# The first attention unit moved into the last block of the input projection

## The chip, the core and the metric

The kernel runs on one core of a Trainium2 chip. The time is the device time of one execution in microseconds; a smaller one is better. Engines: PE is TensorE (PEld its weight loads), DVE is VectorE, ACT is ScalarE, POOL is GpSimd, SP is SyncE, which here only issues DMAs.

## What is computed

One trunk layer of a diffusion model for 512 latent and 128 context tokens with 2048 channels: an input projection of 4608 columns, differential attention (8 heads) and grouped-query attention (8 heads on 2 key heads), an output projection, and 16 experts chosen by the experts. What matters here is the projection and the attention:

```python
p = jnp.einsum('bnd,de->bne', h, w_in)
dq, dk, dv, gq, gk, gv = jnp.split(p, splits, axis=-1)
gq = rmsnorm(gq.reshape(b, n, N_GQA_HEADS, HEAD_DIM), qn_g)
...
a1 = jax.nn.softmax(jnp.einsum('bqhd,bkhd->bhqk', qb1, k1).astype(jnp.float32) * scale, axis=-1)
a2 = jax.nn.softmax(jnp.einsum('bqhd,bkhd->bhqk', qb2, k2).astype(jnp.float32) * scale, axis=-1)
a = (a1 - lam * a2).astype(v.dtype)
return jnp.einsum('bhqk,bkhd->bqhd', a, v)
```

## The kernel before

The tokens are five tiles of 128 (four latent, `TL = 4`, and one of context). The **input projection** runs over nine blocks of 512 columns in the order `ORDER = [8, 2, 3, 4, 0, 1, 6, 7, 5]`: keys first, then queries; block 5, the last, holds values. A block has 16 steps `k`, one for each 128 input channels. A step is 15 matmuls: for each of the five token tiles three products of high and low parts (`three_products`), added up in PSUM banks 0 to 4. Bank 5 serves sums of the conditioning, banks 6 and 7 take transpositions in turn (`xp_bank`).

After a block, ScalarE copies the five banks to `prow` (`block_out`; for block 5 to `V`). VectorE shapes these rows: for blocks 6 to 8 it first sums squares (`mean_squares`, step kind "squares"), GpSimd turns the sums into `rg` by a power, and then `shape_rows` scales and rotates tile by tile (step kind "shape") and counts `roped`. TensorE transposes the shaped rows, four heads of a tile at a time (step kind "rows", line 992), and ScalarE copies them into `qT` or `kT` (line 1435). All of this is laid out by hand in one list of steps, `make_steps()`, that each engine walks through in its own order, with semaphores between them. In block `o`, "shape" of the former block's tile `t` stands at step `2t + 1`, and "rows" of tile `t` follows step `6 + 2t`:

```python
            if o > 0 and ORDER[o - 1] in ROWS_BLOCKS and k >= 6 and k % 2 == 0:
                steps.append(("rows", ORDER[o - 1], (k - 6) // 2))
```

TensorE waits for `roped` ahead of these transpositions. The weights of the projection come in pieces of four steps by SyncE (line 795), are rounded by ScalarE (line 1407) and completed by VectorE (line 2018, "split"); the last piece is asked for after step 7 of the last block.

**Attention** has 68 units, differential (even) and grouped-query ones (odd) in turn. A unit is: `scores` (TensorE, line 1025), `maxima` (VectorE, lines 2047 and 2048), `exps` (ScalarE, line 1454, two for a differential unit), `combine` (VectorE, lines 2083 to 2087, which joins the two maps; 2079 for the others), `prob_transposes` (TensorE, lines 1039 and 1044, into banks 5 and 6), a copy (ScalarE, lines 1507 and 1509), and `values` (TensorE, line 1063, into bank 7). Scores of differential units lie in banks 0 to 3, those of the others in banks 3 and 4. Scores stand two units ahead:

```python
            pe.wait_ge(proj_taken, NT * len(ORDER))
            pe.wait_ge(mod_copied, len(GROUPS))
            scores(0)
            scores(1)
            for u in range(UNITS):
                if u + 2 < UNITS:
                    scores(u + 2)
                ...
                if u >= 1:
                    values(u - 1)
                prob_transposes(u)
```

`scores(u)` from unit 2 on waits until the exponentials of unit `u - 2` are done. The exponentials of unit 0 go to `E`, whose first half lies over two of the three places of the rounded weights.

Of the kernel before, what the change touches and what calls it, by code (L numbers as in the profile page):

```python
# [41 lines left out]
P = 128  # L42
# [56 lines left out]
RAW_AT = {3: (0,), 4: (1,), 5: (2,), 6: (3, 4)}  # L99
ROUTER_AT = {5: (0,), 7: (1, 2)}  # L100
# [63 lines left out]
def make_steps():  # L164
# [37 lines left out]
    for o, b in enumerate(ORDER):  # L202
        for k in range(12 if o == 0 else 0, KC):
# [24 lines left out]
            if o > 0 and ORDER[o - 1] in ROWS_BLOCKS and k >= 6 and k % 2 == 0:  # L228
                steps.append(("rows", ORDER[o - 1], (k - 6) // 2))
# [54 lines left out]
def build(nc, a, laid, outs):  # L284
# [6 lines left out]
    with ctx:  # L291
# [417 lines left out]
        def unit(u):  # L709
            t, j = SEQ[u]  # L710
            nc_, keys = (2 if j < DH else 1), (LAT + PAST if t < TL else 4 * CTX)
            kh = j if j < DH else DH + (j - DH) // GRP
            scale = (DQ if j < DH else HD) ** -0.5
            return t, j, nc_, keys, kh, scale

        def is_diff(u):
            return SEQ[u][1] < DH

        def is_four(u):
            return SEQ[u][0] == TL  # L720

        def four_heads(u):
            return range(SEQ[u][1], SEQ[u][1] + 4)
# [4 lines left out]
        def four_scores(u):  # L728
            n = 8 if is_diff(u) else 4
            return S_ps(u, 0, CTX * n).rearrange("p (h k) -> p h k", k=CTX)  # L730
# [27 lines left out]
        def S_ps(u, c, keys):  # L758

            at0 = S_STEP * c if is_diff(u) else 3 * NB  # L760
            return ps[:, at0:at0 + keys]

        def S_both(keys):
            return ps[:, 0:2 * S_STEP].rearrange("p (c k) -> p c k", c=2)[:, :, 0:keys]
# [103 lines left out]
        def _(pe):  # L868
# [5 lines left out]

            pe.wait_ge(ident_ready, 1)
            for step in STEPS:
                kind = step[0]
                if kind == "cvec":
# [117 lines left out]
            def four_scored(u):  # L996
                _, _, comps, _, _, _ = unit(u)
                qs, ks = slice(P * TL, P * NT), slice(LAT + PAST, LAT + PAST + CTX)
                for i, j in enumerate(four_heads(u)):
                    for c in range(comps):  # L1000
                        rows = slice(0, HD) if comps == 1 else slice(DQ * c, DQ * (c + 1))
                        mm = pe.matmul(four_scores(u)[:, 4 * c + i, :], qT[rows, j, qs], kT[rows, key_head(j), ks],
                                       start=True, stop=True, skip_group_check=True)
                mm.then_inc(scored, 1)

            def scores(u):
                t, j, comps, keys, kh, _ = unit(u)
                if u >= 2:
                    pe.wait_ge(exp_done, u - 1)
                if is_four(u):  # L1010
                    four_scored(u)
                    return
                k0 = 0
                qs = slice(P * t, P * (t + 1))
                if comps == 1:
                    parts = [(0, 0, LAT), (0, LAT, keys)]
                else:

                    parts = [(0, LAT, keys), (1, LAT, keys), (0, 0, 384), (1, P, LAT), (0, 384, LAT), (1, 0, P)]
                for n, (c, lo, hi) in enumerate(parts):  # L1020
                    if n == 5:

                        pe.wait_ge(tail_scored, TAILS[u])
                    rows = slice(0, HD) if comps == 1 else slice(DQ * c, DQ * (c + 1))
                    mm = pe.matmul(S_ps(u, c, keys)[:, lo:hi], qT[rows, j, qs], kT[rows, kh, k0 + lo:k0 + hi],  # L1025
                                   start=True, stop=True, skip_group_check=True)
                    if n == 0 and comps == 2:
                        mm.then_inc(tail_scored, 1)
                mm.then_inc(scored, 1)

# [46 lines left out]
            was_taken(pe, XP_TOTAL - 2)  # L1077
            was_taken(pe, XP_TOTAL - 1)
            pe.wait_ge(proj_taken, NT * len(ORDER))
            pe.wait_ge(mod_copied, len(GROUPS))  # L1080
            scores(0)
            scores(1)
            for u in range(UNITS):
                if u + 2 < UNITS:
                    scores(u + 2)
                if u in OT_AT:
                    pe.wait_ge(pt_copied, u)
                    out_transposes(*OT_AT[u], bank(6))
# [3 lines that stand above are left out]
# [249 lines left out]
        def _(act):  # L1341
# [32 lines left out]

            for step in STEPS:
                kind = step[0]
                if kind == "lam":
# [67 lines left out]
            def exps(u):  # L1445
                t, j, comps, keys, _, scale = unit(u)
                act.wait_ge(max_done, u + 1)
                if u >= 2:
                    act.wait_ge(pt_done, u - 1)
                if is_four(u):  # L1450
                    act.activation(four_probs(u), four_probs(u), ACT.Exp, scale=scale).then_inc(exp_done, 1)
                    return
                for c in range(comps):
                    ins = act.activation(E[:, u % 2, c, 0:keys], S_ps(u, c, keys), ACT.Exp,
                                         bias=nmax[:, u % 4, c:c + 1], scale=scale,
                                         accum_out=ssum[:, u % 4, c:c + 1])
                ins.then_inc(exp_done, 1)

# [36 lines left out]
            exps(0)  # L1495
# [307 lines left out]
        def _(dve):  # L1803
# [115 lines left out]

            for step in STEPS:  # L1920
                kind = step[0]
                if kind == "half":
# [115 lines left out]
            def maxima(u):  # L2038
                t, j, comps, keys, _, scale = unit(u)
                dve.wait_ge(scored, u + 1)  # L2040
                if u >= 1:
                    dve.wait_ge(max_done, u)
                if is_four(u):
                    link(dve.tensor_reduce(four_stats(u)[0], four_scores(u), AX, ALU.max))
                    return
                S = S_both(keys) if comps == 2 else S_ps(u, 0, keys).rearrange("p (c k) -> p c k", c=1)
                link(dve.tensor_reduce(mx[:, 0:comps], S, AX, ALU.max))  # L2047
                dve.tensor_scalar(nmax[:, u % 4, 0:comps], mx[:, 0:comps], -scale, None, ALU.mult).then_inc(max_done, 1)

            def four_shifted(u):  # L2050

                dve.wait_ge(pt_done, u - 1)
                dve.tensor_tensor(four_probs(u), four_scores(u), bc(four_stats(u)[0], CTX, 2), ALU.subtract)\
                    .then_inc(max_done, 1)

            def four_combine(u):

                probs = four_probs(u)
                _, total, inverse, factor = four_stats(u)
                dve.wait_ge(exp_done, u + 1)  # L2060
                dve.wait_ge(probs_ready, u)
                link(dve.tensor_reduce(total, probs, AX, ALU.add))
                if not is_diff(u):
                    dve.reciprocal(inverse, total).then_inc(probs_ready, 1)
                    return
                link(dve.reciprocal(inverse, total))
                link(dve.scalar_tensor_tensor(out=factor, in0=total[:, 0:4], scalar=neglam[:, 0:1], in1=inverse[:, 4:8],
                                              op0=ALU.mult, op1=ALU.mult))
                link(dve.tensor_tensor(probs[:, 4:8, :], probs[:, 4:8, :], bc(factor, CTX, 2), ALU.mult))
                dve.tensor_tensor(probs[:, 0:4, :], probs[:, 0:4, :], probs[:, 4:8, :], ALU.add).then_inc(probs_ready, 1)  # L2070

            def combine(u):
                t, j, comps, keys, _, _ = unit(u)
                if is_four(u):
                    four_combine(u)
                    return
                dve.wait_ge(exp_done, u + 1)
                if comps == 1:
                    dve.reciprocal(rsum[:, u % 4, 0:1], ssum[:, u % 4, 0:1]).then_inc(probs_ready, 1)
                    return  # L2080
                if u >= 1:
                    dve.wait_ge(probs_ready, u)
                link(dve.reciprocal(rsum[:, u % 4, :], ssum[:, u % 4, :]))
                link(dve.scalar_tensor_tensor(out=coef[:, :], in0=ssum[:, u % 4, 0:1], scalar=neglam[:, 0:1],
                                              in1=rsum[:, u % 4, 1:2], op0=ALU.mult, op1=ALU.mult))

                dve.scalar_tensor_tensor(out=E[:, u % 2, 0, 0:keys], in0=E[:, u % 2, 1, 0:keys], scalar=coef[:, 0:1],
                                         in1=E[:, u % 2, 0, 0:keys], op0=ALU.mult, op1=ALU.add).then_inc(probs_ready, 1)

# [37 lines left out]
            maxima(0)  # L2127
            maxima(1)
            combine(0)
# [368 lines left out]
```

## Time and profile before

| | us |
|---|---|
| median of 3 runs | 2104.59 |
| lowest, highest | 2102.16, 2107.1 |
| the profiled execution | 2109.96 |
| its span in the trace | 2108.1 |
| TensorE busy | 2029.9 (96%) |
| VectorE, ScalarE busy | 1140.6, 478.1 |
| mean granted clock of TensorE | 0.989 |

The span runs from the first to the last instruction; the execution's own time is 1.9 us longer. Projection and attention are the first 810 us; the output projection and the routing follow until about 1090, then the experts to the end. An engine's idle time counts only where TensorE stands for it. A row of a timeline gives the start, the duration of one instruction or of a merged group, the engine, the line, and in brackets the idle time before it with what ended it. Matmuls overlap: one of 512 columns lasts 0.39 us, and the next starts 0.23 later. A granted clock of 1.00 is 2.4 GHz, one of 0.50 is 1.2 GHz.

### The profile page before, as it was taken

The page shows a single profiled execution, that of the slowest core. Times are in us where ns is not written, and L with a number is a line of the kernel's source. Part 1 is how long each engine was busy: PE and PEld are TensorE (multiplying, and loading weights), DVE is VectorE, ACT ScalarE, POOL GpSimd, SP SyncE. Part 2 cuts the span into 40 slices and gives each one's busy share as a digit, 9 for nine tenths or more (in the row PEclk, how much of TensorE's full clock was granted, in tenths as well). Part 3 has the DMA queues.
Part 4 walks back from the last instruction along what each step waited for, and adds up shares of the span by engine and source line. Part 5 has one row for each costly group of instructions (what it writes and reads, how often), then busy time and mean ns, then how long its engine had stood idle before and what let it go on. Part 6 is the DMA issues. An engine that isn't in the chain of part 4 may idle for free. (4 is left out here: it accounts for less than half of the span.)

```text
span 2108.1 us, 37671 instructions
## 1 busy us (share of the span) xinstructions
PE 2029.9 (96%) x15045; PEld 1128.7 (54%) x15045; DVE 1140.6 (54%) x2673; ACT 478.1 (23%) x846; POOL 163.3 (8%) x236
## 2 busy tenths in 40 slices
PE   6999999999999999999979999999999999999995
PEld 3578888787878887888842333333333333333331
DVE  4369988997448877777355342333233333223314
ACT  4232222222247776221210000000000000000003
POOL 1020011111000001111120000000000000000001
PEclk9999999999999999999989999999999999999998
DMA  9955567562220005656489999999999999999997
GB/s 389 410 181 219 215 229 259 198 219 101 80 103 1 1 2 221 226 182 207 146 306 378 404 412 418 416 416 425 422 416 416 418 416 414 430 415 417 417 394 312
DMA packets 71924, 614.03 MB, mean 291 GB/s; under 512 B 8432, under 2 KB 10104, under 8 KB 29104
## 3 DMA queue, kind: packets, MB, share of 16 engines
q1 hardware_dynamic: 47392, 514.36, 59.1%
q0 software_dynamic: 18672, 84.89, 12.8%
q10 hardware_dynamic: 5776, 13.63, 1.9%
q8 instruction: 56, 0.92, 0.2%
q14 instruction: 28, 0.23, 0.0%
HBM read 583.28 MB, written 29.60 MB: 291 GB/s over the span
## 5 line engine op out<-in xcount | busy, mean ns | idle before, releaser
L1250 PE MATMUL ps<-arena 128*32 128x512 f32 x6144 | 662.6, 592 | 0.2 <-DVE arena L2301 0.2
L1250 PEld LDWEIGHTS ps<-arena 128*32 128x32 f32 x6144 | 199.4, 110 | 458.3 <-issue 457.7
L1277 PE MATMUL ps<-arena 128*32 128x512 f32 x3072 | 332.8, 592 | 3.7 <-DMA arena<-in_w_expert 1.9
L697 PE MATMUL ps<-B_w_hi,B_x_hi 128*128 128x512 f32 x720 | 287.0, 399 | 6.2 <-DVE B_x_lo L2030 3.3
L699 PE MATMUL ps<-B_w_lo,B_x_hi 128*128 128x512 f32 x720 | 281.5, 391 | 0.0
L698 PE MATMUL ps<-B_w_hi,B_x_lo 128*128 128x512 f32 x720 | 281.3, 391 | 0.0
L1277 PEld LDWEIGHTS ps<-arena 128*32 128x32 f32 x3072 | 99.6, 110 | 234.1 <-issue 227.7
L2333 DVE COPY arena<-arena 128x16 f32 x1200 | 157.3, 182 | 99.9 <-issue 99.1
L2309 DVE TENSOR_TENSOR arena<-ps,arena 64x256 f32<-64x256 f32 x96 | 39.9, 416 | 295.9 <-ACT arena L1605 295.2
L1605 ACT ACTIVATE arena<-ps 64x512 f32<-64x512 f32 x48 | 28.5, 593 | 608.8 <-PE ps L1250 608.8
L697 PEld LDWEIGHTS ps<-B_w_hi,B_x_hi 128*128 128x128 f32 x720 | 135.5, 188 | 47.3 <-issue 12.7
L699 PEld LDWEIGHTS ps<-B_w_lo,B_x_hi 128*128 128x128 f32 x720 | 135.5, 188 | 29.1
L698 PEld LDWEIGHTS ps<-B_w_hi,B_x_lo 128*128 128x128 f32 x720 | 135.8, 189 | 26.7
L1900 DVE SCALAR_TENSOR_TENSOR arena<-arena,cT 128x2048 f32<-128x2048 f32 x60 | 138.2, 2345 | 2.3 <-DMA arena<-in_w_mod 2.3
L1407 ACT ACTIVATE B_w_hi<-arena 128x1024 fp32r<-128x1024 f32 x72 | 75.5, 1058 | 264.7 <-DMA arena<-in_w_in_b 237.3
L2345 DVE COPY arena<-ps 16x512 f32<-16x512 f32 x30 | 20.8, 692 | 208.4 <-PE ps L1277 208.2
L697 PE MATMUL ps<-D_w_hi,D_oT_hi 128*128 128x512 f32 x320 | 126.8, 396 | 0.2 <-DVE D_oT_lo L2125 0.2
L699 PE MATMUL ps<-D_w_lo,D_oT_hi 128*128 128x512 f32 x320 | 124.9, 390 | 0.0
L2018 DVE TENSOR_TENSOR B_w_lo<-arena,B_w_hi 128x1024 fp32r<-128x1024 f32 x72 | 87.7, 1219 | 68.5 <-ACT B_w_hi L1407 68.3
L698 PE MATMUL ps<-D_w_hi,D_oT_lo 128*128 128x512 f32 x320 | 124.6, 390 | 0.0
L2185 DVE SCALAR_TENSOR_TENSOR arena<-arena,cT 128x512 f32<-128x512 f32 x120 | 82.6, 745 | 29.2 <-DMA arena<-in_w_mod 29.1
L2047 DVE TENSOR_REDUCE mx<-ps 128x2 f32<-128x1280 f32 (+1 forms) x64 | 74.0, 1156 | 44.8 <-PE ps L1025 44.1
(286 smaller groups left out, 1964.9 us busy)
## 6 DMA issues: line engine op xcount, KB each, us to landing
arena<-in_w_expert SPq DMA_DIRECT2D x192, 2048.0 KB, 13.9
arena<-in_w_in_b SPq DMA_DIRECT2D x36, 1024.0 KB, 4.9
arena<-in_w_mod_q SPq DMA_DIRECT2D x32, 1024.0 KB, 19.2
arena<-in_w_mod POOLq DMA_DIRECT2D x32, 1024.0 KB, 5.6
arena<-in_w_mod POOLq DMA_DIRECT2D x32, 512.0 KB, 4.6
arena<-in_w_out_b SPq DMA_DIRECT2D x16, 1024.0 KB, 7.0
arena<-in_w_mod POOLq DMA_DIRECT2D x64, 256.0 KB, 3.5
arena<-in_x_sample SPq DMA_DIRECT2D x8, 1024.0 KB, 10.2
```

The costliest lines, as they stand in the source:

```text
L697: eng.matmul(out, x_hi, w_hi, start=start, stop=False)
L698: eng.matmul(out, x_lo, w_hi, start=False, stop=False)
L699: return eng.matmul(out, x_hi, w_lo, start=False, stop=stop)
L1250: mm = pe.matmul(bank(g)[32 * q:32 * q + 32, :], e_rows, w[q], start=start, stop=stop, skip_group_check=True)
L1277: mm = pe.matmul(bank(b)[32 * q:32 * q + 32, :], hT[g][:, f, :], w_four[q], start=f == 0, stop=f == 7, skip_group_check=True)
L1407: act.activation(w_hi, raw, ACT.Copy).then_inc(w_hi_ready, 1)
L1900: ins = dve.scalar_tensor_tensor(out=macs[:, v, :], in0=at(where, D), scalar=cT[:, k, v:v + 1], in1=macs[:, v, :], op0=ALU.mult, op1=ALU.add)
L2018: dve.tensor_tensor(w_lo, raw, w_hi.bitcast(F32), ALU.subtract).then_inc(w_lo_ready, 1)
L2047: link(dve.tensor_reduce(mx[:, 0:comps], S, AX, ALU.max))
L2185: ins = dve.scalar_tensor_tensor(out=late_acc[:, v, :], in0=piece, scalar=cT[:, k, v:v + 1], in1=late_acc[:, v, :], op0=ALU.mult, op1=ALU.add)
L2309: ins = dve.tensor_tensor(hid[g][64 * c:64 * (c + 1), :], bank(g)[0:64, cs], sg[g][0:64, cs], ALU.mult)
L2333: ins = dve.tensor_copy(xstage[:, :, c + i:c + i + 1], x1_cols[:, bass.ds(place, 1), :].rearrange("p o k -> p k o"))
```

## The change

`first_unit`, a new kind of step, stands after step 13 (`FIRST_UNIT_K`) of the last block. There TensorE issues the scores of unit 0, VectorE its maximum and combination, ScalarE its exponentials. The scores of unit 0 go to banks 5 to 7, at the same distance of the two maps as before. So that these banks are free, the transpositions of the former block's rows follow steps 4, 6, ... 12 of the last block; in the other blocks they stay. The functions `four_scored`, `scores`, `exps`, `maxima`, `combine` and their like are moved ahead of the loop over the steps, unchanged. After the block, TensorE transposes the probabilities of unit 0 first, then waits for the bank copies, then issues the scores of units 1 and 2.

```diff
+FIRST_UNIT_K = 13
...
-            if o > 0 and ORDER[o - 1] in ROWS_BLOCKS and k >= 6 and k % 2 == 0:
-                steps.append(("rows", ORDER[o - 1], (k - 6) // 2))
+            first_row = 4 if o == len(ORDER) - 1 else 6
+            if o > 0 and ORDER[o - 1] in ROWS_BLOCKS and k in range(first_row, first_row + 2 * NT, 2):
+                steps.append(("rows", ORDER[o - 1], (k - first_row) // 2))
+            if (o, k) == (len(ORDER) - 1, FIRST_UNIT_K):
+                steps.append(("first_unit",))
...
-            at0 = S_STEP * c if is_diff(u) else 3 * NB
+            at0 = (5 * NB if u == 0 else 0) + S_STEP * c if is_diff(u) else 3 * NB
...
-        def S_both(keys):
-            return ps[:, 0:2 * S_STEP].rearrange("p (c k) -> p c k", c=2)[:, :, 0:keys]
+        def S_both(u, keys):
+
+            at0 = S_STEP - LAT - P if u == 0 else 0
+            from_ = 5 * NB - at0 if u == 0 else 0
+            return ps[:, from_:from_ + 2 * S_STEP].rearrange("p (c k) -> p c k", c=2)[:, :, at0:at0 + keys]
...
+                if kind == "first_unit":
+                    was_taken(pe, XP_TOTAL - 2)
+                    was_taken(pe, XP_TOTAL - 1)
+                    pe.wait_ge(mod_copied, len(GROUPS))
+                    scores(0)
...
-            was_taken(pe, XP_TOTAL - 2)
-            was_taken(pe, XP_TOTAL - 1)
+            prob_transposes(0)
             pe.wait_ge(proj_taken, NT * len(ORDER))
-            pe.wait_ge(mod_copied, len(GROUPS))
-            scores(0)
             scores(1)
-            for u in range(UNITS):
+            scores(2)
+            for u in range(1, UNITS):
...
+                if kind == "first_unit":
+                    after_products(act, len(ORDER) - 1, FIRST_UNIT_K)
+                    exps(0)
...
-            exps(0)
             for u in range(UNITS):
...
+                if kind == "first_unit":
+                    maxima(0)
+                    combine(0)
...
-            maxima(0)
             maxima(1)
-            combine(0)
```

## Rows read from the trace of the kernel before

**Rows 1.** Busy time by stretch (us, busy by engine with instructions, PEclk, DMA share, GB/s).

```profile
core 0: us, PE busy (x) PEld busy (x) DVE busy (x) ACT busy (x) POOL busy (x), PEclk, DMA share, GB/s
...
599.08:611.33 12.25, 9.09 (x53) 6.48 (x52) 6.90 (x14) 5.81 (x15) 1.14 (x2) 0.86 0.42 139
611.33:805.00 193.67, 192.97 (x1519) 160.43 (x1519) 156.91 (x324) 140.34 (x357) 9.08 (x9) 1.00 0.01 1
```

**Rows 2.** TensorE timeline, last block: step 5 begins; rows after 6, 8; last matmul.

```profile
559.27 0.39 PE L697 MATMUL ps<-B_w_hi,B_x_hi 128*128 128x512 f32 x1
...
566.07 0.60 PE L992 MATMUL ps<-ident,arena 128*128 128x128 f32 x4
...
573.35 0.60 PE L992 MATMUL ps<-ident,arena 128*128 128x128 f32 x4
...
598.85 0.39 PE L699 MATMUL ps<-B_w_lo,B_x_hi 128*128 128x512 f32 x1
```

**Rows 3.** Timelines of GpSimd, VectorE and ScalarE in the same block.

```profile
557.07 4.43 POOL L1646 TENSOR_TENSOR rg<-ssg,mhalf 128x20 f32<-128x20 f32 x1 [52.56 <-DVE ssg L1835]
...
563.76 0.69 DVE L1868 TENSOR_TENSOR arena<-arena 128x512 f32<-128x512 f32 x1
...
579.32 0.69 DVE L1868 TENSOR_TENSOR arena<-arena 128x512 f32<-128x512 f32 x1
...
574.97 1.06 ACT L1407 ACTIVATE B_w_hi<-arena 128x1024 fp32r<-128x1024 f32 x1 [7.66 <-DMA arena<-in_w_in_b]
```

**Rows 4.** Timelines of VectorE and TensorE in the block before it, tile 0.

```profile
506.76 0.69 DVE L1868 TENSOR_TENSOR arena<-arena 128x512 f32<-128x512 f32 x1
...
507.60 0.63 PE L992 MATMUL ps<-ident,arena 128*128 128x128 f32 x4 [0.39 <-DVE arena L1868]
```

**Rows 5.** Timeline of all engines where attention begins.

```profile
600.12 2.64 PE L1025 MATMUL ps<-arena 64*128 64x128 f32 x16 [0.89 <-ACT arena L1357]
...
601.59 1.49 DVE L2047 TENSOR_REDUCE mx<-ps 128x2 f32<-128x1280 f32 x1 [19.12 <-PE ps L1025]
...
603.32 0.79 ACT L1454 ACTIVATE arena<-ps,nmax 128x640 f32<-128x640 f32 x1 [3.45 <-DVE nmax L2048]
...
605.03 2.51 PE L1025 MATMUL ps<-arena 64*128 64x128 f32 x12 [2.27 <-ACT arena L1454]
...
607.47 0.98 PE L1039 MATMUL ps<-ident,arena 128*128 128x128 f32 x4
...
608.40 1.25 PE L1025 MATMUL ps<-arena 128*128 128x512 f32 x4
```

**Rows 6.** Timelines of TensorE and VectorE over one steady pair of units.

```profile
617.26 1.36 PE L1025 MATMUL ps<-arena 64*128 64x128 f32 x12
...
618.55 1.38 PE L1063 MATMUL ps<-arena 128*128 128x128 f32 x10
...
619.77 0.60 PE L1039 MATMUL ps<-ident,arena 128*128 128x128 f32 x4
...
620.32 1.25 PE L1025 MATMUL ps<-arena 128*128 128x512 f32 x4
...
621.40 1.32 PE L1063 MATMUL ps<-arena 128*128 128x128 f32 x10
...
621.60 0.82 DVE L2047 TENSOR_REDUCE mx<-ps 128x1 f32<-128x640 f32 x1 [0.91 <-PE ps L1025]
...
622.46 0.15 DVE L2048 TENSOR_SCALAR nmax<-mx 128x1 f32<-128x1 f32 x1
...
623.20 1.14 PE L1025 MATMUL ps<-arena 64*128 64x128 f32 x8
```

**Rows 7.** Busy time in single microseconds at the beginning of attention.

```profile
605.00:606.00 1.00, 0.97 (x6) 0.93 (x8) 0.92 (x3) 0.75 (x2) 0.00 (x0) 0.50 0.60 242
```

**Rows 8.** TensorE in the routing stage: timeline, and busy time of one stretch.

```profile
1079.82 1.03 PE L1212 MATMUL ps<-ident,arena 64*64 64x16 f32 x8 [9.27 <-DVE arena L2258]
...
1082.63:1086.05 3.42, 3.42 (x18) 3.42 (x18) 1.74 (x9) 0.00 (x0) 2.45 (x4) 0.50 0.25 53
```

More of the change, by code:

```diff
@@ L873, in xp_bank, with four_scored, scores @@
                 return bank(6 + i % 2)
+            def four_scored(u):
+                _, _, comps, _, _, _ = unit(u)
+                qs, ks = slice(P * TL, P * NT), slice(LAT + PAST, LAT + PAST + CTX)
+                for i, j in enumerate(four_heads(u)):
+                    for c in range(comps):
+                        rows = slice(0, HD) if comps == 1 else slice(DQ * c, DQ * (c + 1))
+                        mm = pe.matmul(four_scores(u)[:, 4 * c + i, :], qT[rows, j, qs], kT[rows, key_head(j), ks],
+                                       start=True, stop=True, skip_group_check=True)
+                mm.then_inc(scored, 1)
+            def scores(u):
+                t, j, comps, keys, kh, _ = unit(u)
+                if u >= 2:
+                    pe.wait_ge(exp_done, u - 1)
+                if is_four(u):
+                    four_scored(u)
+                    return
+                k0 = 0
+                qs = slice(P * t, P * (t + 1))
+                if comps == 1:
+                    parts = [(0, 0, LAT), (0, LAT, keys)]
+                else:
+                    parts = [(0, LAT, keys), (1, LAT, keys), (0, 0, 384), (1, P, LAT), (0, 384, LAT), (1, 0, P)]
+                for n, (c, lo, hi) in enumerate(parts):
+                    if n == 5:
+                        pe.wait_ge(tail_scored, TAILS[u])
+                    rows = slice(0, HD) if comps == 1 else slice(DQ * c, DQ * (c + 1))
+                    mm = pe.matmul(S_ps(u, c, keys)[:, lo:hi], qT[rows, j, qs], kT[rows, kh, k0 + lo:k0 + hi],
+                                   start=True, stop=True, skip_group_check=True)
+                    if n == 0 and comps == 2:
+                        mm.then_inc(tail_scored, 1)
+                mm.then_inc(scored, 1)
             pe.wait_ge(ident_ready, 1)
@@ L877, in _ @@
                 kind = step[0]
-                if kind == "cvec":
+                if kind == "first_unit":
[3 more added lines that the diff above has]
+                    scores(0)
+                elif kind == "cvec":
                     pe.wait_ge(c_in, 32)
@@ L993, in _ @@
                     mm.then_inc(xp_done, 1)
[L996 to L1029, printed above, removed]
             def prob_transposes(u):
@@ L1373, in block_out, with exps @@
                             act.dma_start(dv_d[P * t:P * (t + 1), :], prow[:, t, :]).then_inc(val_out, 16)
+            def exps(u):
+                t, j, comps, keys, _, scale = unit(u)
+                act.wait_ge(max_done, u + 1)
+                if u >= 2:
+                    act.wait_ge(pt_done, u - 1)
+                if is_four(u):
+                    act.activation(four_probs(u), four_probs(u), ACT.Exp, scale=scale).then_inc(exp_done, 1)
+                    return
+                for c in range(comps):
+                    ins = act.activation(E[:, u % 2, c, 0:keys], S_ps(u, c, keys), ACT.Exp,
+                                         bias=nmax[:, u % 4, c:c + 1], scale=scale,
+                                         accum_out=ssum[:, u % 4, c:c + 1])
+                ins.then_inc(exp_done, 1)
             for step in STEPS:
                 kind = step[0]
-                if kind == "lam":
+                if kind == "first_unit":
+                    after_products(act, len(ORDER) - 1, FIRST_UNIT_K)
+                    exps(0)
+                elif kind == "lam":
                     act.wait_ge(lam_sum, 1)
@@ L1442, in _ @@
                                    ACT.Copy).then_inc(xp_taken[i % 2], 1)
[L1445 to L1457, printed above, removed]
             def take_ot(i, b):
@@ L1918, in half_sum, with maxima @@
                     ins.then_inc(mac_done[v], 1)
+            def maxima(u):
+                t, j, comps, keys, _, scale = unit(u)
+                dve.wait_ge(scored, u + 1)
+                if u >= 1:
+                    dve.wait_ge(max_done, u)
+                if is_four(u):
+                    link(dve.tensor_reduce(four_stats(u)[0], four_scores(u), AX, ALU.max))
+                    return
+                S = S_both(u, keys) if comps == 2 else S_ps(u, 0, keys).rearrange("p (c k) -> p c k", c=1)
+                link(dve.tensor_reduce(mx[:, 0:comps], S, AX, ALU.max))
+                dve.tensor_scalar(nmax[:, u % 4, 0:comps], mx[:, 0:comps], -scale, None, ALU.mult).then_inc(max_done, 1)
@@ new lines, in four_shifted, with four_combine @@
+            def four_shifted(u):
+                dve.wait_ge(pt_done, u - 1)
+                dve.tensor_tensor(four_probs(u), four_scores(u), bc(four_stats(u)[0], CTX, 2), ALU.subtract)\
+                    .then_inc(max_done, 1)
+            def four_combine(u):
+                probs = four_probs(u)
+                _, total, inverse, factor = four_stats(u)
+                dve.wait_ge(exp_done, u + 1)
+                dve.wait_ge(probs_ready, u)
+                link(dve.tensor_reduce(total, probs, AX, ALU.add))
+                if not is_diff(u):
+                    dve.reciprocal(inverse, total).then_inc(probs_ready, 1)
+                    return
+                link(dve.reciprocal(inverse, total))
+                link(dve.scalar_tensor_tensor(out=factor, in0=total[:, 0:4], scalar=neglam[:, 0:1], in1=inverse[:, 4:8],
+                                              op0=ALU.mult, op1=ALU.mult))
+                link(dve.tensor_tensor(probs[:, 4:8, :], probs[:, 4:8, :], bc(factor, CTX, 2), ALU.mult))
+                dve.tensor_tensor(probs[:, 0:4, :], probs[:, 0:4, :], probs[:, 4:8, :], ALU.add).then_inc(probs_ready, 1)
@@ new lines, in combine @@
+            def combine(u):
+                t, j, comps, keys, _, _ = unit(u)
+                if is_four(u):
+                    four_combine(u)
+                    return
+                dve.wait_ge(exp_done, u + 1)
+                if comps == 1:
+                    dve.reciprocal(rsum[:, u % 4, 0:1], ssum[:, u % 4, 0:1]).then_inc(probs_ready, 1)
+                    return
+                if u >= 1:
+                    dve.wait_ge(probs_ready, u)
+                link(dve.reciprocal(rsum[:, u % 4, :], ssum[:, u % 4, :]))
+                link(dve.scalar_tensor_tensor(out=coef[:, :], in0=ssum[:, u % 4, 0:1], scalar=neglam[:, 0:1],
+                                              in1=rsum[:, u % 4, 1:2], op0=ALU.mult, op1=ALU.mult))
+                dve.scalar_tensor_tensor(out=E[:, u % 2, 0, 0:keys], in0=E[:, u % 2, 1, 0:keys], scalar=coef[:, 0:1],
+                                         in1=E[:, u % 2, 0, 0:keys], op0=ALU.mult, op1=ALU.add).then_inc(probs_ready, 1)
@@ L1920, in _ @@
             for step in STEPS:
                 kind = step[0]
-                if kind == "half":
+                if kind == "first_unit":
+                    maxima(0)
+                    combine(0)
+                elif kind == "half":
                     half_sum(step[1])
@@ L2035, in _ @@
                     shape_rows(step[1], step[2])
[L2038 to L2088, printed above, removed]
```

## The prediction

> **What bounds the kernel now.** I read the engine shares first, then the busy time by stretch, then the timelines around the edit. The page gives TensorE 96% of the span, so what moves the end is time in which TensorE stands or runs at half clock. By stretch there is one such place at the edit: in the 12.25 us from the end of the last projection step to the scores of unit 4, TensorE is busy for 9.09 us at a mean granted clock of 0.86, while over the rest of attention it is busy for 192.97 of 193.67 us [rows 1]. In the last projection block itself it does not wait once: step follows step every 3.40 us ((566.07 - 559.27) / 2), with four transpositions of the former block's rows between some of them [rows 2]. So whatever is put into that block is paid in full, unless something there is removed, and any wait there is new time.
>
> **Boundary, before.** The last product is issued at 598.85, so the block ends at 599.08 (one matmul pitch is 0.23). scores(0) waits for the copies out of the five banks and starts at 600.12. The maximum starts at 601.59, the exponentials at 603.32, and scores(2), which waits for the exponentials of unit 0, starts at 605.03 [rows 5]. scores(0) and scores(1) are issued in 1.29 + 1.08 = 2.37 us at full clock [rows 6], so TensorE stands from 602.49 to 605.03. Idle in all: 1.04 + 2.54 = 3.58 us. The clock is at 0.50 from 605 on [rows 7]: scores(2) takes 2.44 instead of 1.29 us, the transpositions of unit 0 0.93 instead of 0.55 [rows 5, 6]. That is 1.53 us more. Idle and clock together are 5.1 of the 12.25 us.
>
> **Boundary, after.** I lay the new order out from the same durations, with the block's end still written as 599.08. Transpositions of unit 0: to 599.63. Wait for the bank copies, as before: to 600.12. scores(1): to 601.20. scores(2), free of its wait, since exponentials 0 are done: to 602.49. scores(3) waits for the exponentials of unit 1: maximum from 601.40, 1.01 us with its scaling, exponential from about 602.44, 0.85 long ((605.03 - 603.32) / 2), so scores(3) starts at about 603.38 and ends at 604.46. Values of unit 0 and transpositions of unit 1 (1.22 + 0.60) bring it to 606.28. scores(4) needs exponentials 2: the maximum of unit 2 starts at 602.49 + 0.18, the exponentials 1.73 later, done 1.71 after that, at 606.1 [rows 5, 6]. So scores(4) starts at 606.28 and the steady beat of 5.94 us a pair follows. From block's end to scores(4): 7.20 us, against 12.25. scores(0) is moved, not removed: inside the block it costs its 1.29 us and I add 0.1 for its seams. **Gain: 12.25 - 7.20 - 1.39 = 3.7 us.** It rests on the clock staying up, with 0.49 + 0.89 = 1.4 us idle in place of 3.58.
>
> **What the moved unit does in the block.** Same 12 matmul records, one maximum, two exponentials, one combination; other banks (5 to 7), same shapes. After step 13 come 6.8 us of products; the chain of unit 0 takes 0.18 + 1.73 + 1.71 us to the exponentials and about 1.3 to the combination, 4.9 in all, so it is hidden, with 1.9 us to spare. ScalarE is done at 3.6 us, before the first bank is ready for copying at about 4.3 (3.40 + 0.68 + latency), so the copies queued behind the exponentials are not late. VectorE has nothing else queued there. The waits added on TensorE (two copies of turned rows, the last modulation copy) have long been met: the last rows now come after step 12, a whole step earlier. SyncE's loads of V and of the output weights hang on steps 11 and 15 and only move with them; GpSimd's stores likewise.
>
> **The rows steps.** To make room, the five transposition steps of block 7's rows move from after steps 6, 8, ... 14 to after steps 4, 6, ... 12. This is the term that decides. The rows of tile 0 must be shaped first, and this chain does not hang on TensorE at that point: GpSimd raises the mean squares to a power from 557.07 to 561.50, VectorE shapes behind it, and its last addition runs 563.76 to 564.45 [rows 3]. The transpositions started at 566.07, 1.6 us later, without a wait. After the change their place is the end of step 4, 559.27 [rows 2]. They can start at 564.60: in the block before, the same handoff, with its transpositions after step 6, is just reached, TensorE waits 0.39 us and starts 0.15 after the addition ends (506.76 + 0.69 = 507.45, start 507.60) [rows 4]. So TensorE stands for 564.60 - 559.27 = **5.33 us**, with steps 5 and on queued behind it. Nothing gives it back: no later wait in the block can shrink, since there is none. The other tiles are in time: tile 3, the closest, is shaped 10.06 us after the end of step 7 (579.32 + 0.69, against 573.35 - 3.40 = 569.95), because its shaping queues behind a weight piece that lands 5.02 us after that step [rows 2, 3]; its new place comes 3 x 3.40 + 0.48 = 10.68 after it (0.48 is what four transpositions add, 573.35 - 566.07 - 2 x 3.40). With 0.15 for the start that leaves some 0.5 us; a slower landing would add up to about 1 us.
>
> **The clock after that wait** is not shown by the trace of before at this place. Lower bound: after idle of 1.04 and 2.54 us the clock fell once and cost 1.53 us [rows 5, 7]. Upper bound: after a 9.27 us wait in the routing stage it stays at 0.50 from 1079.82 to 1086.05 with TensorE at work again [rows 8], 6.2 us of which half, 3.1 us, is lost. The wait of 5.33 lies between; nearer to the first, so I take **2.0 us**. (Zero is excluded: the idle here is longer than the one that made it fall.)
>
> **Sum:** + 5.33 + 2.0 - 3.7 = **+3.6 us**. The profiled execution took 2109.96 us (span 2108.1 and 1.9 around it) and would take 2113.6; it lay 5.4 above the median of the runs. I put the same difference on the median: 2104.6 + 3.6 = **2108.2 us**. The stages behind attention start later by the same amount and have no load that is timed from anything earlier.
>
> **Rivals.** (A, my forecast, chance 0.62) as above, +2.5 to +5 us. (B, 0.08) The clock is hardly lower after the wait, contrary to the rows: +5.3 + 0.2 - 3.7 = +1.8. (C, 0.14) A further loss: the clock falls again at the start of attention, where two idle pieces remain (1.53), or tile 3's rows are late (up to 1): +4.6 to +6. For: the two pieces lie within 4.3 us. Against: 1.4 us is much less than 3.58. (D, the other side, 0.10) No wait at tile 0: the shaping is ready in time, and only the gain is left, 2104.6 - 3.7 = 2100.9 us. It decides if tile 0's last addition ends by about 559.1, 5.3 us earlier than in the trace; GpSimd's power alone ends at 561.50 [rows 3], so it needs a misreading of mine. (E, 0.06) The change does not do what it says: unit 0 is ahead, but scores(3) hangs on unit 1's exponentials by the same chain, and the stand of 2.54 us is only passed on. Then only the first 1.04 us and part of the clock are won, about 2: +5.3. Against: in the layout scores(2) and the transpositions fill that chain's time.
>
> For C a rule speaks beside the rows. Transpositions of unit 0 run between the two idle pieces, and in the steady beat, with ten transpositions a pair, the clock stays at 1.00 [rows 1]. The Trainium skill, "TensorE: Matmul & The Clock Gate", Part 4, says that a transposition does not count as busy for the clock as a matmul does. By it the idle at the start of attention would look like 2.0 instead of 1.4 us, still below 3.58; were it to make the clock fall, the sum would be +5.1. The trace can't show it at this place; it is part of why C has 0.14.
>
> **Chances.** A measurement of this kernel tells some 0.2%, 4.2 us, from no change. A lies across that bound: of its 0.62 I give 0.38 to within and 0.24 to slower. B is within. C: 0.02 within, 0.12 slower. D is a gain of 0.18%: 0.06 within, 0.04 faster. E slower. Together faster 0.04, within 0.54, slower 0.42. Range: A, B and C with the spread of the runs of before (2102.2 to 2107.1, about 2.5 to a side) give 2104.2 to 2112.0; D is left out below.
>
> **What would show it.** Right: the transpositions of block 7's first rows start with an idle of about 5.3 us released by VectorE's last shaping addition, and the clock is at half for some us behind it; the exponentials of unit 0 lie inside the block; scores(2) follows scores(1) without a wait; from block's end to scores(4) 7.2 us. Wrong: no wait there (D); a low clock again at the start of attention or a wait at tile 3's rows (C); 2 us or more of idle before scores(3) (E).

## The result

| | us |
|---|---|
| before, median of 22 runs | 2105.22 (2101.86 to 2109.29) |
| changed, median of 22 runs | 2110.20 (2106.91 to 2115.41) |
| ratio | 1.0020, interval 1.0014 to 1.0026 |
| forecast | 2108.2 (2104.2 to 2112.0) |

The change makes the kernel slower by 0.20%, 4.2 us by the ratio (2.9 to 5.5); + 3.6 was forecast. The forecast's 2108.2 stands on 2104.59, the median of the three runs of before that were at hand; over 22 runs it is 2105.22. In the profiled execution TensorE waits at the place that the forecast names, and for what it names. Timeline of TensorE, then VectorE and GpSimd, in the last projection block of the changed kernel (start, duration, engine, line, operation, in brackets the idle time before and what ended it); the lines answer to [rows 2] and [rows 3]:

```profile
555.00 0.39 PE L703 MATMUL ps<-B_w_lo,B_x_hi 128*128 128x512 f32 x1
...
560.47 1.02 PE L1039 MATMUL ps<-ident,arena 128*128 128x128 f32 x4 [5.08 <-DVE arena L1880]
...
569.38 0.60 PE L1039 MATMUL ps<-ident,arena 128*128 128x128 f32 x4
```

```profile
552.94 4.43 POOL L1658 TENSOR_TENSOR rg<-ssg,mhalf 128x20 f32<-128x20 f32 x1 [52.47 <-DVE ssg L1847]
...
559.63 0.69 DVE L1880 TENSOR_TENSOR arena<-arena 128x512 f32<-128x512 f32 x1
```

The last product of step 4 is issued at 555.00, so the step ends at 555.23. VectorE's last addition for tile 0 runs 559.63 to 560.32, and the transpositions start 0.15 us behind it. By starts the wait is 5.24 us. The next transpositions follow 8.91 us after these, where [rows 2] has 7.28 for the same work. The busy time by stretch (columns as in [rows 1]; the clock is the number behind POOL) shows why: the clock is at half behind the wait.

```profile
561.40:562.40 1.00, 1.00 (x4) 0.81 (x4) 0.96 (x3) 0.60 (x1) 0.00 (x0) 0.50 0.06 16
562.40:563.40 1.00, 1.00 (x3) 0.73 (x3) 1.00 (x3) 0.00 (x0) 0.00 (x0) 0.50 0.00 0
563.40:564.40 1.00, 1.00 (x5) 0.80 (x4) 0.74 (x2) 0.00 (x0) 0.00 (x0) 0.71 0.00 0
603.43:610.64 7.21, 6.28 (x42) 4.35 (x40) 3.90 (x9) 4.17 (x11) 1.14 (x2) 1.00 0.73 236
```

The last of these lines is the beginning of attention, from the block's end to the scores of unit 4: 7.21 us at a clock of 1.00, against 12.25 us at 0.86 in [rows 1]. Its timeline, with the moved unit's scores ahead of it, answers to [rows 5]:

```profile
595.20 1.36 PE L911 MATMUL ps<-arena 64*128 64x128 f32 x12
...
596.61 1.49 DVE L1941 TENSOR_REDUCE mx<-ps 128x2 f32<-128x1280 f32 x1 [10.89 <-PE ps L911]
...
598.40 0.80 ACT L1394 ACTIVATE arena<-ps,nmax 128x640 f32<-128x640 f32 x1 [5.94 <-DVE nmax L1942]
...
600.55 0.88 DVE L1981 SCALAR_TENSOR_TENSOR arena<-arena,coef 128x640 f32<-128x640 f32 x1
...
603.43 0.60 PE L1051 MATMUL ps<-ident,arena 128*128 128x128 f32 x4
...
604.27 2.64 PE L911 MATMUL ps<-arena 128*128 128x512 f32 x16
...
607.70 1.35 PE L911 MATMUL ps<-arena 128*128 128x512 f32 x4 [0.79 <-ACT arena L1394]
...
610.64 1.36 PE L911 MATMUL ps<-arena 64*128 64x128 f32 x12
```

Unit 0 is scored at 595.20, its maximum starts at 596.61, the combination ends at 601.43, 2.0 us before its transpositions at 603.43. Scores of units 1 and 2 then run in one piece (x16), and scores(3) stands 0.79 us for the exponentials of unit 1.

Spans don't show the difference: the changed kernel's profiled execution has 2106.9 us, the one before 2108.1. Both kernels are the same up to the last block, yet GpSimd's power (the one instruction that turns the sums of squares into `rg`) starts at 552.94 in one and at 557.07 in the other. So I compare traces by one stretch, **from the start of GpSimd's power in the last block (line 1646 before) to the first matmul of the scores of unit 4**. It holds all that the change touches. Before: 611.33 - 557.07 = 54.26 us. Changed: 610.64 - 552.94 = 57.70. Difference: + 3.44 us. The measure is not exact: over the traces of this case step 4 of the last block ends 2.00 to 2.34 us after the power starts, so two stretches compare to some 0.3 us.

### The profile page after: what moved, and what is told of

Its sections match the earlier page's. It is cut to its first block and busy times, and to the rows that moved or that the text cites. A ratio compares the mean times of both kernels' runs of the same rounds, so it can differ in the third digit from the quotient of the medians.

```text
span 2106.9 us, 37670 instructions
## 1 busy us (share of the span) xinstructions
PE 2030.2 (96%) x15045; PEld 1130.2 (54%) x15045; DVE 1139.4 (54%) x2673; ACT 478.3 (23%) x846; POOL 163.6 (8%) x236
```

## The experiments

All times are ratios to the kernel before, run on the same chip; "stretch" is the one just defined.

| kernel | rows after steps | unit 0 | stretch, us | ratio (95% interval) | us by the ratio |
|---|---|---|---|---|---|
| before | 6 8 10 12 14 | behind the block | 54.26, 54.44 | | |
| changed | 4 6 8 10 12 | in the block | 57.70, 57.41 | 1.0020 (1.0014 to 1.0026); again 1.0012 (1.0002 to 1.0021) | + 4.2; + 2.5 |
| f1 | 4 6 8 10 12 | behind | 61.33 | 1.0047 (1.0034 to 1.0060) | + 9.9 |
| f2 | 6 7 8 10 12 | in | 50.81 | 0.9981 (0.9973 to 0.9990) | - 4.0 |
| f3 | 5 7 8 10 12 | in | 54.27 | 0.9998 (0.9988 to 1.0007) | - 0.4 |
| f4 | 6 7 8 10 12 | behind | 52.93 | 1.0005 (0.9996 to 1.0015) | + 1.1 |
| g1 | 4 6 8 10 12, wait filled | in | 56.03 | 0.9997 (0.9988 to 1.0006) | - 0.6 |

### f1: the rows' steps alone

```diff
-            if o > 0 and ORDER[o - 1] in ROWS_BLOCKS and k >= 6 and k % 2 == 0:
-                steps.append(("rows", ORDER[o - 1], (k - 6) // 2))
+            row_steps = (4, 6, 8, 10, 12) if o == len(ORDER) - 1 else (6, 8, 10, 12, 14)
+            if o > 0 and ORDER[o - 1] in ROWS_BLOCKS and k in row_steps:
+                steps.append(("rows", ORDER[o - 1], row_steps.index(k)))
```

> The kernel before with one part of the change alone: in the last block the transpositions of the former block's rows follow steps 4, 6, 8, 10 and 12; the first unit stays behind the block. Theory (the loss is the wait for tile 0's shaping): a wait of about 5.2 us before the first of these transpositions and a lower clock behind it for some 1.5 to 2 us, nothing gained, so 6.5 to 7.5 us slower than before. Rival (the rows steps are harmless and the moved unit itself costs what is lost): no change. Rival (the later stages soak the wait up): a wait of 5 us in the trace, but less than 3 us in the time.

Slower by 9.9 us (7.2 to 12.6); the stretch is 7.07 us longer than before (61.33 - 54.26). TensorE's timeline in the block and where attention begins:

```profile
563.54 1.09 PE L993 MATMUL ps<-ident,arena 128*128 128x128 f32 x4 [5.16 <-DVE arena L1869]
...
572.52 0.60 PE L993 MATMUL ps<-ident,arena 128*128 128x128 f32 x4
...
606.09 2.64 PE L1026 MATMUL ps<-arena 64*128 64x128 f32 x16 [0.89 <-ACT arena L1358]
...
611.00 1.60 PE L1026 MATMUL ps<-arena 64*128 64x128 f32 x8 [2.27 <-ACT arena L1455]
...
612.00:613.00 1.00, 1.00 (x7) 0.48 (x5) 0.32 (x1) 0.00 (x0) 0.00 (x0) 0.50 0.02 8
```

The same wait (5.16) and the same slow piece behind it (8.98 us to the next transpositions, 1.70 more than 7.28), and at the start of attention the old idle pieces of 0.89 and 2.27 with the clock at half behind them (last line). So the rows' steps alone cost what the forecast gave to them, 5.3 + 2.0 = 7.3; both rivals fall. The measured time is above that (five runs): its interval only begins where the trace's 7.07 lies, the trace shows nothing for the rest, and I leave it open.

### f2: unit 0 in the block, each tile's rows where they are ready

The edit is that of f1 on the changed kernel, with `row_steps = (6, 7, 8, 10, 12)`: tile 0 waits two steps longer, tile 1 follows a step behind it, the other three stay where the change has them.

> The changed kernel with the rows' transpositions of the last block after steps 6, 7, 8, 10 and 12, so that each comes after its tile is shaped and all five still lie ahead of the first unit after step 13. Theory: no wait at tile 0 (shaped 1.5 us before its place), none at tile 1 (1.6 us before), the moved unit's gain alone is left, 3.5 to 3.7 us faster than before, and 7.2 us from the block's end to the scores of unit 4. Rival (the moved unit costs): no faster than before, or slower. Rival (the wait only moves on to tile 1 or 2): idle of 1 us or more there, at most 2.5 us faster.

Faster by 4.0 us (2.1 to 5.7). The wait is gone, and the moved unit's gain is left: 54.26 - 50.81 = 3.45 us in the stretch. Timeline of TensorE, tiles 0 to 2, the scores of unit 0, and attention's beginning:

```profile
563.50 0.60 PE L1039 MATMUL ps<-ident,arena 128*128 128x128 f32 x4
...
567.38 0.60 PE L1039 MATMUL ps<-ident,arena 128*128 128x128 f32 x4
...
571.27 0.60 PE L1039 MATMUL ps<-ident,arena 128*128 128x128 f32 x4
...
589.80 1.36 PE L911 MATMUL ps<-arena 64*128 64x128 f32 x12
...
598.02 0.60 PE L1051 MATMUL ps<-ident,arena 128*128 128x128 f32 x4
...
598.87 2.64 PE L911 MATMUL ps<-arena 128*128 128x512 f32 x16
...
602.30 1.35 PE L911 MATMUL ps<-arena 128*128 128x512 f32 x4 [0.79 <-ACT arena L1394]
...
605.24 1.36 PE L911 MATMUL ps<-arena 64*128 64x128 f32 x12
```

None of the three transpositions has a bracket, that is, none waits. From the block's end at 598.02 to the scores of unit 4 it is 7.22 us. By medians this kernel takes 2100.44 us, the kernel before on the same chip 2105.91.

### f4: the same rows' steps, unit 0 behind the block

Edit of f1 with `row_steps = (6, 7, 8, 10, 12)`.

> The kernel before with the rows' transpositions of the last block after steps 6, 7, 8, 10 and 12 and the first unit where it was, as the control of the kernel with both. Theory: no wait and no change of time, 0 us; the 3.6 us of the other kernel then belong to the moved unit alone. Rival (pulling rows forward gains or loses by itself, through ScalarE or VectorE): 1 us or more to either side.

No change that can be measured (-0.04% to +0.15%). That interval reaches to 3 us and can't exclude the rival's 1 us; the trace can: from GpSimd's power to the first scores of attention it is 597.35 - 554.25 = 43.10 us, before 600.12 - 557.07 = 43.05. Pulled forward to where they are ready, the rows cost nothing, so f2's gain belongs to the moved unit. The trace holds one surprise, by which the stretch is 52.93 and not 54.26 us. Timeline of GpSimd and TensorE, and busy time at the start of attention; the second block is the kernel before:

```profile
554.25 4.43 POOL L1647 TENSOR_TENSOR rg<-ssg,mhalf 128x20 f32<-128x20 f32 x1 [52.52 <-DVE ssg L1836]
...
597.35 2.64 PE L1026 MATMUL ps<-arena 64*128 64x128 f32 x16 [0.89 <-ACT arena L1358]
...
602.26 1.36 PE L1026 MATMUL ps<-arena 64*128 64x128 f32 x12 [2.27 <-ACT arena L1455]
...
602.26:607.18 4.92, 4.90 (x37) 3.78 (x37) 4.04 (x9) 3.27 (x9) 0.00 (x0) 1.00 0.13 51
```

```profile
605.03:611.33 6.30, 6.30 (x36) 4.80 (x36) 4.24 (x10) 3.39 (x9) 0.00 (x0) 0.75 0.09 36
```

The idle pieces are those of before (0.89 and 2.27), but the clock stays at 1.00 behind them: scores(2) to scores(4) take 4.92 us where the kernel before takes 6.30 at 0.75. Against this one trace the moved unit is worth only 52.93 - 50.81 = 2.1 us. The times don't bear that out: the medians of f4 and f2, on one chip, lie 5.9 us apart (2106.35 and 2100.44), and f4 is not faster than before. So the clock that stayed up was probably not the rule in f4's runs, which no run shows; why the times of these two kernels lie further apart than their traces, by 2.1 or 3.5 us, stays open.

### f3: a short wait on purpose

Edit of f2 with `row_steps = (5, 7, 8, 10, 12)`.

> As the last kernel, with tile 0's transpositions after step 5 instead of 6: a wait of about 1.85 us is made on purpose. Theory: the wait is paid one for one, and if the clock's share needs a long idle, the clock stays up: 1.9 - 3.7 = -1.8 us against before. If a lower clock follows a short idle too: about 0 us. Rival (waits in the block are not paid in full): as fast as the last kernel.

As fast as before: f2's gain is spent. The stretch is 54.27 - 50.81 = 3.46 us longer than f2's.

```profile
559.25 0.39 PE L703 MATMUL ps<-B_w_lo,B_x_hi 128*128 128x512 f32 x1
...
561.61 0.91 PE L1039 MATMUL ps<-ident,arena 128*128 128x128 f32 x4 [1.97 <-DVE arena L1880]
...
570.54 0.60 PE L1039 MATMUL ps<-ident,arena 128*128 128x128 f32 x4
...
562.00:563.00 1.00, 1.00 (x5) 0.90 (x4) 1.00 (x2) 0.45 (x1) 0.00 (x0) 0.50 0.06 16
563.00:564.00 1.00, 1.00 (x3) 0.73 (x3) 0.96 (x3) 1.00 (x2) 0.00 (x0) 0.50 0.00 0
```

The wait is 1.97 us by the profile's bracket; by starts it is 2.13 (step 5 ends at 559.25 + 0.23 = 559.48), where 1.85 was expected. The clock adds 1.65 us: it fell to 0.50 behind this short wait too, and to the next transpositions it takes 8.93 us (two steps and four transpositions, 7.28 at full clock). Together that is 3.78, of which the stretch shows 3.46: here step 5 ends 5.40 us after GpSimd's power starts, in f2 5.67. My own reading, that the clock's share needs a long idle, was wrong; of the two outcomes written down it is the second.

### g1: the wait filled with work, and both kernels once more

In the changed kernel, ahead of the wait for tile 0:

```diff
+                    if (blk, t) == (7, 0):
+                        pe.wait_ge(mod_copied, len(GROUPS))
+                        x_hi, (_, w_hi, _) = parts_B["x_hi"][4], half_b(8 * (len(ORDER) - 1) + 2)
+                        for _ in range(22):
+                            pe.matmul(bank(5), x_hi[:, 0:P], w_hi[:, 0:NB], start=True, stop=True)
```

> The changed kernel with 22 extra products of one 128x512 tile each, into the free bank 5, issued after step 4 ahead of the wait for tile 0's shaping (some 22 x 0.23 = 5.0 us of work whose result nobody reads). Theory (the loss is a wait of 5.2 us plus a lower clock that follows from standing idle): TensorE still gets to tile 0's transpositions at the same moment, but the clock stays up, so from GpSimd's power to the scores of unit 4 it takes 56.1 instead of 57.7 us, and the time is 1.5 to 2 us below the changed kernel's. Rival (the lower clock there comes from something else than the idle): the same time as the changed kernel, a granted clock of 0.5 behind the transpositions.

> The changed kernel itself once more, beside the one with the filled wait. Expected: a wait of 5.1 us at tile 0, one or two low stretches of the clock behind it, 57.5 to 59.2 us from GpSimd's power to the scores of unit 4, 0.2% slower than before. If the clock's share is a fixed 1.6 us, 57.7 again.

> The kernel before itself once more, for the clock at the start of attention: in its first trace the clock fell there, in the control with early rows it did not. If the fall there is a matter of chance from one execution to the next, it is absent here or present again with the same idle of 0.89 and 2.27 us: 52.9 or 54.3 us from GpSimd's power to the scores of unit 4. The moved unit's gain is then 2.1 us in some executions and 3.5 in others, not 3.7 always.

TensorE of g1, then the changed kernel again:

```profile
555.03 5.15 PE L1038 MATMUL ps<-B_w_hi,B_x_hi 128*128 128x512 f32 x22
...
560.13 0.66 PE L1044 MATMUL ps<-ident,arena 128*128 128x128 f32 x4
...
567.46 0.60 PE L1044 MATMUL ps<-ident,arena 128*128 128x128 f32 x4
...
560.13:567.46 7.33, 7.33 (x35) 6.08 (x35) 5.81 (x9) 1.66 (x2) 0.00 (x0) 1.00 0.00 0
```

```profile
565.68 1.09 PE L1039 MATMUL ps<-ident,arena 128*128 128x128 f32 x4 [5.15 <-DVE arena L1880]
...
574.31 0.60 PE L1039 MATMUL ps<-ident,arena 128*128 128x128 f32 x4
```

In g1 the 22 products reach to 560.13, the transpositions begin as late after GpSimd's power as ever (7.44 us; 7.53 in the changed kernel), and the clock is at 1.00 behind them: 7.33 us to the next ones instead of 8.91. The stretch is 56.03 us, as expected (56.1). So the lower clock comes from standing idle, not from the place. In time g1 is at 2106.44 beside 2109.83 of the changed kernel; each is compared with the kernel before alone, and the two intervals overlap a little (from 1.0002 to 1.0006). The 3.4 us between the medians have the sign that the theory asks for, but are more than the 1.5 to 2 us expected and than the traces' 1.4 to 1.7, so they are no size to build on. Work that nobody reads makes a kernel less slow here; it is a test, not a remedy.

The changed kernel again has 8.63 us where its first trace has 8.91: the clock's share is 1.35 us in one execution and 1.63 in the other, and its stretch of 57.41 lies just below the 57.5 to 59.2 expected. The kernel before again has its clock fall at the start of attention (stretch 54.44). With f1 that is three traces in which it fell behind the pieces of 0.89 and 2.27, and one, f4, in which it did not. What decides is not settled; the idle before it is the same in all four.

## Why the prediction was right

- **The wait at tile 0's rows** (5.33 us): 5.24 in the trace (5.31 in f1 and in the second trace of the changed kernel), ended by VectorE's last addition as in the text, paid in full (f1), and gone when the rows stand where they are ready (f2).
- **The clock behind it** (2.0 us, bounds 1.5 and 3.1): 1.63, 1.35 and 1.70 us in three traces; f1 and both traces of the changed kernel. The bound from below was the better value, and one trace lies under it: one fall costs about what it did at the start of attention, 6.30 - 4.92 = 1.38 us there by f4, not the 1.53 that the forecast took from steady units. The sentence that the wait "lies between" the two ends by its length was a poor guide; f3 loses 1.65 us behind a wait of 2.13.
- **The gain at the boundary** (3.7 us): 3.45 in f2 against the trace of before. The layout's 7.20 us from block's end to scores(4) is 7.21, but two small misses cancel in it: scores(1) starts 0.84 us after the block's end (604.27 - 603.43), not 1.04, and the wait before scores(3) is 1.06 us by starts (607.70 - 604.27 - 2.37), not 0.89. The seam was mis-sized: scores(0) in the block costs 1.50 us (f2: 598.02 - 585.84 = 12.18 from tile 4's transpositions to the block's end, less 3 x 3.40 + 0.48), not 1.39. A part of the gain was luck of the trace: where the clock does not fall, as in f4, the stretch with unit 0 behind the block is 52.93 us and moving the unit is worth 2.1. The forecast took that fall for certain in the kernel before.
- **The other tiles** had no wait, tile 3 neither, in spite of its 0.5 us; the chain of unit 0 was hidden with 2.0 us to spare (1.9 forecast).
- **The sum** (+3.6): 5.24 + 1.63 - 3.45 = 3.42, against 3.44 in the stretch. The parts add up across kernels: f2's 50.81 and the two terms give 57.68, the changed kernel has 57.70, closer than the measure can promise. That + 3.6 came so near is in part luck: the clock's term was 0.4 too large and the gain 0.25 too large, and the two errors cancel. The range was set a little inside its own terms: B with 2.5 us of spread reaches down to 2103.9, C up to 2113.1.
- **Rivals.** B (clock hardly lower) falls by three traces, C (a second fall in attention) by the clock of 1.00 there, in all five traces with unit 0 in the block, though transpositions lie between the two idle pieces; what the rule of the Trainium skill on transpositions ("TensorE: Matmul & The Clock Gate", Part 4) would have added did not come. D falls by the wait, E by the 7.21 us. The first comparison's + 4.2 us lies on the bound of 4.2 itself, the second's + 2.5 within it, so the measured times don't decide between within and slower, to which the forecast gave 0.54 and 0.42.

## What to carry to other kernels

Ask of every step that is pulled forward in a hand-written order what produces its input, and when: here a move by two steps ran into a chain of GpSimd and VectorE that was done 1.6 us before the old place, while the other four tiles had room. Move each by its own slack, not all by one number: the same idea with one list of steps changed turns +4.2 us into -4.0. On an engine that is never idle, a wait costs its length, and some 1.5 us more can be lost to half clock behind it, here even behind a wait of 2 us.

## What the runs showed of the hardware

- After a wait of 1.97 us TensorE's clock went to half (0.50, 1.2 GHz) for some 3 us, though it had been busy before and was busy behind it (f3). The clock's fall was paid with 1.35 to 1.70 us, whether the wait was 1.97 or 5.16 us long.
- A low clock costs only while TensorE works. In f1 it is at 0.50 from 561 on, 2.5 us before the transpositions start at 563.54, and that part of it costs nothing:

```profile
562.00:563.00 1.00, 0.00 (x0) 0.00 (x0) 0.97 (x4) 0.00 (x0) 0.00 (x0) 0.50 0.00 0
```

- A wait of 1.42 us in the block before, between the same kind of products, left the clock at 1.00 (kernel before; timeline, then busy time around the wait):

```profile
503.47 0.50 PE L697 MATMUL ps<-B_w_hi,B_x_hi 128*128 128x512 f32 x1 [1.42 <-DVE B_w_lo L2018]
502.00:503.50 1.50, 0.08 (x2) 0.03 (x1) 1.42 (x2) 1.06 (x1) 1.50 (x1) 1.00 0.00 0
503.50:505.00 1.50, 1.50 (x7) 1.22 (x8) 0.36 (x1) 0.00 (x0) 1.01 (x1) 1.00 0.00 0
```

- At half clock a product of a 128x512 tile follows the last after 0.42 us in the changed kernel, at full clock after 0.22 to 0.23:

```profile
561.71 0.63 PE L702 MATMUL ps<-B_w_hi,B_x_lo 128*128 128x512 f32 x1
562.13 0.63 PE L703 MATMUL ps<-B_w_lo,B_x_hi 128*128 128x512 f32 x1
...
564.61 0.39 PE L701 MATMUL ps<-B_w_hi,B_x_hi 128*128 128x512 f32 x1
564.83 0.40 PE L702 MATMUL ps<-B_w_hi,B_x_lo 128*128 128x512 f32 x1
```

- With the same idle pieces of 0.89 and 2.27 us the clock fell in three executions and stayed up in one.
- Stretches that are the same program differ by microseconds from one execution to the next: GpSimd's power in the last block starts between 552.69 and 558.15 us. A change of 4 us can't be read from two spans.
